# Dense products that read the moving operand's columns alternately from its two halves, with evictions that restore the order

## The chip, the cores and the metric

One core of one Trainium2 chip runs the whole program. The metric is device time of one launch in microseconds, the median of several runs. The core has a matrix engine (TensorE), VectorE, ScalarE and GpSimd, an SBUF of 128 partitions, and a PSUM of 8 banks of 512 fp32 columns in each partition, into which TensorE accumulates.

## The reference

One inference step of one decoder layer, for a prompt of 256 tokens and for 8 sample tokens with the same weights, all in float32:

```
x += 0.5 * SwiGLU_1(RMSNorm(x))                 # 2048 -> 5632 -> 2048
h  = RMSNorm(x);  P = h @ w_in                  # 2048 -> 6400
attention, RWKV-7 time mixing, short convolution, each on its columns of P
x += concat(B_out, A_out, C_out) @ w_out        # 2048 -> 2048
x += 0.5 * SwiGLU_2(RMSNorm(x))
SwiGLU(h) = (silu(h @ w_gate) * (h @ w_up)) @ w_down
```

The outputs are x and the new states. Nearly all arithmetic is in the products with w_gate, w_up, w_down (twice), w_in and w_out; below they are called the dense products.

## The kernel before, in words

Activations lie transposed: a feature is a partition, a token is a column. The 256 prompt tokens and the 8 sample tokens form one row of N = 264 columns. `xr` holds x as 16 tiles of 128 x 264.

Precision is kept by splitting. A weight chunk of up to 4 x 128 rows and 256 columns is loaded into `raw` by SyncE; ScalarE rounds it to `wH` (float32r, L310), VectorE forms the rest `wL = raw - wH` (L365). The activations are split in the same way into `xH`, `xL` (L413, L421), `hH`, `hL` (L473, L477) and `mixH`, `mixL`. A dense product is then three float32r matmuls for each weight tile of 128 x 128: `wH` with the high part (L378), `wH` with the low part (L379), `wL` with the high part (L380). All read 264 moving columns and add into 264 columns of one PSUM bank. `products` issues one chunk: four tiles of rows times two halves of the 256 columns times three, 24 matmuls. The first chunks of w_out go through `ahead_product` (L339) with buffers of their own.

Both functions read the moving operand and write PSUM through views with step -1: the last token first. Since input and output are both reversed, every token still lands in its own column.

Four chunks in ring buffers separate loading, rounding and multiplying; a chunk's consumers wait on the counting semaphores `landed`, `head_made`, `tail_made` and `chunk_used`. All loops are written out by hand for each engine, and an engine works in the order in which its code is written.

Results leave PSUM on VectorE two banks (528 columns) at a time: `gate_scale` (L458) and `hidden` (L466) multiply gate and up by the norm factor `rs`, `project` (L712) does so for w_in's columns into `pj`, `x_add` (L430) adds w_down's and w_out's results to `xr`, and `y_add` (L696) forms the final x in `yf`, which TensorE then transposes (L827, L829) for the output. Gate uses banks 0 and 1, up banks 2 and 3; w_in's pairs alternate between 0 and 2, w_down's and w_out's between 4 and 6. TensorE waits for an eviction only before it begins to overwrite the same banks.

The other matmuls named below are the sums over head dimensions at L1183 (plain fp32, 128 x 264) and the picking of sample values at L1276 (128 weight columns, 4 or 6 moving ones). VectorE's small copies at L979, L1060, L1062, L1381 and L1452 bring transposed columns out of PSUM; L1060 writes into `shT` viewed "p r b -> p b r" (r innermost, 8 elements apart), L1062 into `zs` viewed "p r i b -> p b i r" (r innermost, 24 elements apart), L1452 in runs of four. L1808 reads 264 columns of one bank.

Of the kernel before, what the change touches and what calls it, by code (L numbers as in the profile page):

```python
# [20 lines left out]
ALU = mybir.AluOpType  # L21
# [8 lines left out]
N = T + NB  # L30
# [22 lines left out]
OUT_K0 = (0, 12, 4, 8)  # L53
# [57 lines left out]
def build(nc, t, o):  # L111
# [4 lines left out]
    def at(name, shape, dt, off):  # L116

        return nc.alloc_sbuf_tensor_at(name, shape, dt, offset=base + off)
# [5 lines left out]
    xr = at("xr", [P, KT, N], F32, 49152)  # L124
# [6 lines left out]
    gt = at("gt", [P, 2, N], F32, E0)  # L131
    st = at("st", [P, 2, N], F32, E0 + 2112)
    ut = at("ut", [P, 2, N], F32, E0 + 4224)
# [4 lines left out]
    rs = at("rs", [P, N], F32, K0)  # L138
# [16 lines left out]
    yf = at("yf", [P, 2, 2, N], F32, M0 + 92928 + 6144)  # L155
# [6 lines left out]
    pj = at("pj", [P, MT, N], F32, PB)  # L162
# [81 lines left out]
    def inner_slots(*ks):  # L244
# [18 lines left out]
    ahead = {k: (at(f"wH{k}", [P, CK, CW], F32R, hi), at(f"wL{k}", [P, CK, CW], F32R, lo))  # L263
             for k, hi, lo in ((0, F0, F0 + 8192), (1, F0 + 4096, PB + G), (2, L0 + 4 * HB, L0 + 4 * HB + 4096),
                               (3, L0 + 4 * HB + 8192, L0 + 4 * HB + 12288),
                               (6, PB + 2 * G, PB + 2 * G + 4096), (7, PB + 2 * G + 8192, PB + 2 * G + 12288))}
# [7 lines left out]
    ps = ctx.enter_context(nc.psum_tensor("ps", [P, 8, 512], F32))  # L274
    sems = {}

    def S(name):
        if name not in sems:
            sems[name] = ctx.enter_context(nc.semaphore(name))
        return sems[name]  # L280
# [13 lines left out]
    def number(first, per, i, k):  # L294

        return i * per + (first + k)
# [28 lines left out]
    def pe_ahead(pe, k, qs=range(CK)):  # L325

        pe.wait_ge(S("tail_made"), OUT + k + 1)
        for q in qs:
            for half in range(2):
                ahead_product(k, q, half, 0, mixH, k % 4 == 0 and q == 0)  # L330
                ahead_product(k, q, half, 0, mixL)
                last = ahead_product(k, q, half, 1, mixH, stop=k == 7 and q == CK - 1)
        if CK - 1 in qs:
            last.then_inc(S("chunk_used"), 1)

    def ahead_product(k, q, half, part, mix, start=False, stop=False):

        cols = slice(half * P, half * P + P)
        return nc.tensor.matmul(ps[:, 4 + k // 4 * 2 + half, 0:N][:, ::-1], ahead[k][part][:, q, cols],  # L339
                                mix[:, OUT_K0[k % 4] + q, :][:, ::-1], start=start, stop=stop)  # L340

    def pe_ahead_rwkv(pe):

# [18 lines left out]
    def tail(dve, nk, first, per, i, k):  # L362
# [3 lines left out]
                                wH[:, k % RING, 0:nk, :].bitcast(F32), ALU.subtract  # L366
                                ).then_inc(S("tail_made"), 1)

    def products(pe, vH, vL, k0, nk, bank, start, stop, first, per, i, k):

        pe.wait_ge(S("tail_made"), number(first, per, i, k) + 1)
        for q in range(nk):
            for half in range(2):
                cols = slice(half * P, half * P + P)
                out = ps[:, bank + half, 0:N][:, ::-1]
                high, low = vH[:, k0 + q, :][:, ::-1], vL[:, k0 + q, :][:, ::-1]
                a, b = start and q == 0, stop and q == nk - 1
                nc.tensor.matmul(out, wH[:, k % RING, q, cols], high, start=a, stop=False)  # L378
                nc.tensor.matmul(out, wH[:, k % RING, q, cols], low, start=False, stop=False)  # L379
                last = nc.tensor.matmul(out, wL[:, k % RING, q, cols], high, start=False, stop=b)  # L380
        last.then_inc(S("chunk_used"), 1)

    def two(ap):

        return ap[:].unsqueeze(1).broadcast_to([P, 2, N])
# [6 lines left out]
    def early(q):  # L392

        return isinstance(q, int) and q < 2
# [32 lines left out]
    def x_add(dve, w, q, bank, factor, used):  # L427

        dve.wait_ge(S("chunk_used"), used)
        nc.vector.scalar_tensor_tensor(xr[:, bass.ds(q * 2, 2), :], ps[:, bank:bank + 2, 0:N], factor,  # L430
                                       xr[:, bass.ds(q * 2, 2), :], ALU.mult, ALU.add
                                       ).then_inc(S("x_ready"), 1)

    def norm_sum(pe, w):

# [19 lines left out]

    def gate_scale(dve, u, first, p):
        dve.wait_ge(S("chunk_used"), first + 4 + p * GU_PER)
        nc.vector.tensor_tensor(gt[:], ps[:, 0:2, 0:N], two(rs), ALU.mult).then_inc(S("gate_scaled"), 1)  # L458

    def gate_silu(act, u, p):  # L460
        act.wait_ge(S("gate_scaled"), FT // 2 * u + 1 + p)
# [1 line left out]

    def hidden(dve, u, first, p):
        dve.wait_ge(S("chunk_used"), first + GU_PER + p * GU_PER)
        nc.vector.tensor_tensor(ut[:], ps[:, 2:4, 0:N], two(rs), ALU.mult).then_inc(S("up_scaled"), 1)  # L466
        dve.wait_ge(S("up_scaled"), FT // 2 * u + 1 + p)
        dve.wait_ge(S("silu_made"), FT // 2 * u + 1 + p)
        nc.vector.tensor_tensor(hf[:], st[:], ut[:], ALU.mult).then_inc(S("hidden_made"), 1)
# [171 lines left out]
    def dve_ffn(dve, u, gu, dn):  # L641
        def gate_up(i, first_pair):
            for k in range(RING if first_pair and u == 0 else 0, 4):
                tail(dve, CK, gu, GU_PER, i, k)
            if not first_pair:
                hidden(dve, u, gu, i - 1)
            elif u == 1:
                x_add(dve, 2, KT // 2 - 1, 6, 1.0, GU2)
            tail(dve, CK, gu, GU_PER, i, 4)
            if not first_pair:  # L650
                hidden_tail(dve, u, i - 1)
            elif u == 1:
                x_tails(dve, 2, KT // 2 - 1)
            for k in range(5, GU_PER):
                tail(dve, CK, gu, GU_PER, i, k)
            if first_pair:
                norm_reciprocal(dve, 2 * u)
            gate_scale(dve, u, gu, i)
# [32 lines left out]
    def y_add(dve, q, slot, used):  # L691

        dve.wait_ge(S("chunk_used"), used)
        if not early(q):
            dve.wait_ge(S("y_turned"), q - 1)
        nc.vector.scalar_tensor_tensor(yf[:, slot, :, :], ps[:, 4 + 2 * slot:6 + 2 * slot, 0:N], 0.5,  # L696
                                       xr[:, bass.ds(q * 2, 2), :], ALU.mult, ALU.add
                                       ).then_inc(S("x_ready"), 1)

    def column_pair(q):  # L700

# [2 lines left out]
    def seat(q):  # L704

        return 2 * column_pair(q) + (-6 if 16 <= q < 19 else 6 if q >= 22 else 0)

    def project(dve, q, bank):

        dve.wait_ge(S("chunk_used"), IN + IN_PER + q * IN_PER)  # L710
        c = seat(q)
        nc.vector.tensor_tensor(pj[:, c:c + 2, :], ps[:, bank:bank + 2, 0:N], two(rs), ALU.mult  # L712
                                ).then_inc(S("projected"), 1)

    def dve_in(dve):
        for k in range(4):
            tail(dve, CK, IN, IN_PER, 0, k)
        x_add(dve, 1, KT // 2 - 1, 6, 0.5, IN)
        x_tails(dve, 1, KT // 2 - 1)
        for k in range(4):  # L720
# [55 lines left out]
    def pe_ffn(pe, u, gu, dn):  # L776
        w = 2 * u

        def gate_up(i, first_pair):
            for k in range(GU_PER):  # L780
                if first_pair and k < 4:
                    pe.wait_ge(S("x_tail"), 16 * w + 4 * (k + 1))
                if k == 0 and not first_pair:
                    pe.wait_ge(S("gate_scaled"), FT // 2 * u + i)
                if k == 4 and not first_pair:
                    pe.wait_ge(S("up_scaled"), FT // 2 * u + i)
                products(pe, xH, xL, CK * (k % 4), CK, 0 if k < 4 else 2, k % 4 == 0, k % 4 == 3,
                         gu, GU_PER, i, k)
                if first_pair and u == 0 and k == 0:
                    pe_turn_x(pe, 6)  # L790
                    pe_turn_x(pe, 7)
                if first_pair and k == (5 if u == 0 else 3):
                    norm_sum(pe, w)

        def down(i, jj, first_pair):
            q = i * 2 + jj
            if not (isinstance(i, int) and i == 0):
                pe.wait_ge(S("x_ready"), 8 * (w + 1) - 1 + q)
            for k in range(DN_PER):
                if first_pair:  # L800
                    pe.wait_ge(S("hidden_tail"), FT // 2 * u + (DN_K0[k] + DN_KT[k] + 1) // 2)
                products(pe, hH, hL, DN_K0[k], DN_KT[k], 4 + 2 * jj, k == 0, k == DN_PER - 1,
                         dn + DN_PER * jj, 2 * DN_PER, i, k)
                if u == 1 and not first_pair and k == 5:
                    turn_y(pe, q - 1, 1 - jj)
# [26 lines left out]
    def pe_in(pe):  # L832
        for k in range(4):
            pe.wait_ge(S("x_tail"), 16 + 4 * (k + 1))
            products(pe, xH, xL, CK * k, CK, 0, k == 0, k == 3, IN, IN_PER, 0, k)
# [1651 lines left out]
```

## Time and profile before

| | |
|---|---|
| median of 3 runs | 2109.93 us (2109.79 to 2113.65) |
| span of the profiled execution | 2106.7 us |
| TensorE matmul busy | 2074.8 us, 98% |
| VectorE busy | 1183.1 us, 56% |
| ScalarE busy | 880.0 us, 42% |
| GpSimd busy | 196.9 us, 9% |
| mean granted TensorE clock | 0.994 of 2.4 GHz |
| DMA | 373.43 MB, 177 GB/s mean |

The profile is of one execution; its span, from the first to the last instruction, is what sums are made against. Matmuls are pipelined: an instruction's duration is much longer than the distance to the next one's start, and a busy share of 98% says only that there are few gaps. Weight loads (PEld) run beside the matmul before them.

### The profile page before, as it was taken

What the parts mean: (1) busy time and instruction counts of PE and PEld (TensorE: products, weight loads), DVE (VectorE), ACT (ScalarE), POOL (GpSimd) and SP (SyncE); (2) the same over time, 40 slices, a digit from 0 to 9 for tenths busy, and PEclk for the clock granted to TensorE, in tenths of its full rate; (3) what the DMA queues carried; (4) which work ended last, traced back from release to release, by engine and by line L of the source; (5) the groups of instructions that cost most, each with busy time, mean ns of one, the idle gap of its engine ahead of it and who ended that gap; (6) DMA issues with size and microseconds to landing.
All of it is one profiled execution on the core that took longest, in us unless ns stands there. A gap on an engine that the chain in (4) does not pass through costs nothing.

```text
span 2106.7 us, 44887 instructions
## 1 busy us (share of the span) xinstructions
PE 2074.8 (98%) x18520; PEld 2038.6 (97%) x18520; DVE 1183.1 (56%) x1203; ACT 880.0 (42%) x1004; POOL 196.9 (9%) x160
## 2 busy tenths in 40 slices
PE   8999999999999999999998999999999999999999
PEld 7999999999999999999986899999999999999999
DVE  6555555555444545568996575555555555544443
ACT  5444444444434434434345444444444444433333
POOL 4000000000000000015401871000000000000000
PEclk9999999999999999999998999999999999999999
DMA  5655555665555556668873055555556555556553
GB/s 184 197 182 180 179 180 179 185 182 180 176 179 177 187 172 199 175 201 221 238 237 88 4 165 190 180 180 180 181 179 186 179 179 180 183 166 196 185 176 125
DMA packets 361375, 373.43 MB, mean 177 GB/s; under 512 B 13321, under 2 KB 353837, under 8 KB 361190
## 3 DMA queue, kind: packets, MB, share of 16 engines
q1 hardware_dynamic: 352288, 350.53, 53.5%
q0 software_dynamic: 5424, 15.39, 3.1%
q10 hardware_dynamic: 3582, 6.33, 0.9%
q8 instruction: 63, 1.03, 0.2%
q14 instruction: 18, 0.15, 0.0%
HBM read 366.89 MB, written 5.32 MB: 177 GB/s over the span
## 4 chain that ended last, share of the span: by engine, by line
PE 89%; DVE 5%; DMA 3%; ACT 1%; POOL 1%; issue 1%; ACTq 0%; SPq 0%; POOLq 0%; DVEq 0%
PE ps L378 28%; PE ps L380 28%; PE ps L379 28%; DMA raw<-in_w_in_dram 2%; DVE wL L365 2%; DVE wL L323 1%; POOL acc L888 1%; PE ps L1266 1%; PE ps L1955 0%; DMA vb<-in_cache_swa_v_dram 0%; ACT wH L310 0%; PE ps L1958 0%; DMA xin<-in_x_prompt_dram 0%; PE ps L1966 0%; PE ps L339 0%
## 5 line engine op out<-in xcount | busy, mean ns | idle before, releaser
L365 DVE TENSOR_TENSOR wL<-raw,wH 128x1024 fp32r<-128x1024 f32 (+1 forms) x668 | 824.2, 1240 | 829.3 <-ACT wH L310 828.5
L310 ACT ACTIVATE wH<-raw 128x1024 fp32r<-128x1024 f32 (+1 forms) x668 | 691.2, 1037 | 966.4 <-PE ps L380 888.0
L378 PE MATMUL ps<-xH,wH 128*128 128x264 f32 x3616 | 1030.2, 285 | 6.2 <-DVE wL L365 5.8
L380 PE MATMUL ps<-xH,wL 128*128 128x264 f32 x3616 | 1027.3, 284 | 0.0
L379 PE MATMUL ps<-xL,wH 128*128 128x264 f32 x3616 | 1027.2, 284 | 0.0
L378 PEld LDWEIGHTS ps<-xH,wH 128*128 128x128 f32 x3616 | 681.3, 188 | 11.3 <-issue 9.7
L380 PEld LDWEIGHTS ps<-xH,wL 128*128 128x128 f32 x3616 | 681.1, 188 | 0.0
L379 PEld LDWEIGHTS ps<-xL,wH 128*128 128x128 f32 x3616 | 680.5, 188 | 0.2
L378 PE MATMUL ps<-hH,wH 128*128 128x264 f32 x1408 | 402.4, 286 | 0.0
L380 PE MATMUL ps<-hH,wL 128*128 128x264 f32 x1408 | 401.4, 285 | 0.0
L379 PE MATMUL ps<-hL,wH 128*128 128x264 f32 x1408 | 401.3, 285 | 0.0
L378 PEld LDWEIGHTS ps<-hH,wH 128*128 128x128 f32 x1408 | 265.0, 188 | 0.2
L379 PEld LDWEIGHTS ps<-hL,wH 128*128 128x128 f32 x1408 | 265.1, 188 | 0.0
L380 PEld LDWEIGHTS ps<-hH,wL 128*128 128x128 f32 x1408 | 264.6, 188 | 0.0
L462 ACT ACTIVATE st<-gt 128x528 f32<-128x528 f32 x44 | 28.5, 647 | 83.6 <-DVE gt L458 83.6
L888 POOL TENSOR_TENSOR acc<-acc,sq 128x528 f32<-128x528 f32 x21 | 34.9, 1663 | 278.0 <-ACT sq L406 277.0
L378 PE MATMUL ps<-mixH,wH 128*128 128x264 f32 x192 | 54.5, 284 | 0.0
L379 PE MATMUL ps<-mixL,wH 128*128 128x264 f32 x192 | 54.5, 284 | 0.0
L380 PE MATMUL ps<-mixH,wL 128*128 128x264 f32 x192 | 54.5, 284 | 0.0
L890 POOL COPY acc<-sq 128x528 f32<-128x528 f32 x3 | 2.7, 894 | 552.5 <-ACT sq L406 549.7
L421 DVE SCALAR_TENSOR_TENSOR xL<-xr,vcol,xH 128x264 fp32r<-128x264 f32 (+1 forms) x48 | 29.9, 664 | 15.6 <-ACT xH L413 15.4
L380 PEld LDWEIGHTS ps<-mixH,wL 128*128 128x128 f32 x192 | 36.1, 188 | 0.0
(377 smaller groups left out, 1140.3 us busy)
## 6 DMA issues: line engine op xcount, KB each, us to landing
raw<-in_ffn_w_gate_dram SPq DMA_DIRECT2D x176, 512.0 KB, 3.5
raw<-in_ffn_w_up_dram SPq DMA_DIRECT2D x176, 512.0 KB, 3.5
raw<-in_ffn_w_down_dram SPq DMA_DIRECT2D x128, 512.0 KB, 3.3
raw<-in_w_in_dram SPq DMA_DIRECT2D x100, 512.0 KB, 4.9
raw<-in_ffn_w_down_dram SPq DMA_DIRECT2D x64, 384.0 KB, 2.8
raw<-in_w_out_dram SPq DMA_DIRECT2D x32, 512.0 KB, 4.4
kb<-in_cache_swa_k_dram POOLq DMA_DIRECT2D x24, 256.0 KB, 6.6
vb<-in_cache_swa_v_dram ACTq DMA_DIRECT2D x24, 256.0 KB, 6.4
```

Source lines behind the costliest of these rows:

```text
L310: nc.scalar.activation(wH[:, k % RING, 0:nk, :], raw[:, k % RING, 0:nk, :], ACT.Copy).then_inc(S("head_made"), 1)
L323: nc.vector.tensor_tensor(low[:], raw[:, k % RING], high[:].bitcast(F32), ALU.subtract).then_inc(S("tail_made"), 1)
L365: nc.vector.tensor_tensor(wL[:, k % RING, 0:nk, :], raw[:, k % RING, 0:nk, :], wH[:, k % RING, 0:nk, :].bitcast(F32), ALU.subtract).then_i ...
L378: nc.tensor.matmul(out, wH[:, k % RING, q, cols], high, start=a, stop=False)
L379: nc.tensor.matmul(out, wH[:, k % RING, q, cols], low, start=False, stop=False)
L380: last = nc.tensor.matmul(out, wL[:, k % RING, q, cols], high, start=False, stop=b)
L421: nc.vector.scalar_tensor_tensor(xL[:, bass.ds(q * 2 + e, 1), :], xr[:, bass.ds(q * 2 + e, 1), :], vcol[:, 0, bass.ds(q * 2 + (16 * w + e) ...
L462: nc.scalar.activation(st[:], gt[:], ACT.Silu).then_inc(S("silu_made"), 1)
L888: nc.gpsimd.tensor_tensor(acc[:], acc[:], sq[:, slot, :, :], ALU.add).then_inc(S("squares_added"), 1)
L890: nc.gpsimd.tensor_copy(acc[:], sq[:, 0, :, :]).then_inc(S("squares_added"), 1)
L1266: last = nc.tensor.matmul(ps[rows, 4, :], pS[:, g, b, :], vb[:, b % 3, g, :], start=g == 0, stop=g == 2)
```

## The change

Two views replace the reversed ones. The moving operand is read as token 0, token 132, token 1, token 133, and so on; PSUM is written in ascending order, so column 2c + w of a bank holds token 132w + c. Each eviction reads its banks with step 2 and writes natural order. `x_add` and `y_add`, which had one instruction for two banks, now have one for each bank.

```diff
@@ ahead_product
-        return nc.tensor.matmul(ps[:, 4 + k // 4 * 2 + half, 0:N][:, ::-1], ahead[k][part][:, q, cols],
-                                mix[:, OUT_K0[k % 4] + q, :][:, ::-1], start=start, stop=stop)
+        return nc.tensor.matmul(ps[:, 4 + k // 4 * 2 + half, 0:N].rearrange("p (c way) -> p c way", way=2), ahead[k][part][:, q, cols],
+                                two_ways(mix[:, OUT_K0[k % 4] + q, :]), start=start, stop=stop)
@@
+    def two_ways(ap):
+
+        return ap.rearrange("p (way c) -> p c way", way=2)
+
+    def by_token(bank):
+
+        return ps[:, bank:bank + 2, 0:N].rearrange("p e (c way) -> p e way c", way=2)
+
+    def by_way(ap):
+
+        return ap.rearrange("p e (way c) -> p e way c", way=2)
+
@@ products
-                out = ps[:, bank + half, 0:N][:, ::-1]
-                high, low = vH[:, k0 + q, :][:, ::-1], vL[:, k0 + q, :][:, ::-1]
+                out = ps[:, bank + half, 0:N].rearrange("p (c way) -> p c way", way=2)
+                high, low = two_ways(vH[:, k0 + q, :]), two_ways(vL[:, k0 + q, :])
@@ x_add
-        nc.vector.scalar_tensor_tensor(xr[:, bass.ds(q * 2, 2), :], ps[:, bank:bank + 2, 0:N], factor,
-                                       xr[:, bass.ds(q * 2, 2), :], ALU.mult, ALU.add
-                                       ).then_inc(S("x_ready"), 1)
+        for e in range(2):
+            tile = by_way(xr[:, bass.ds(q * 2 + e, 1), :])[:, 0]
+            last = nc.vector.scalar_tensor_tensor(tile, by_token(bank)[:, e], factor, tile, ALU.mult, ALU.add)
+        last.then_inc(S("x_ready"), 1)
@@ gate_scale
-        nc.vector.tensor_tensor(gt[:], ps[:, 0:2, 0:N], two(rs), ALU.mult).then_inc(S("gate_scaled"), 1)
+        nc.vector.tensor_tensor(by_way(gt[:]), by_token(0), by_way(two(rs)), ALU.mult).then_inc(S("gate_scaled"), 1)
@@ hidden
-        nc.vector.tensor_tensor(ut[:], ps[:, 2:4, 0:N], two(rs), ALU.mult).then_inc(S("up_scaled"), 1)
+        nc.vector.tensor_tensor(by_way(ut[:]), by_token(2), by_way(two(rs)), ALU.mult).then_inc(S("up_scaled"), 1)
@@ y_add
-        nc.vector.scalar_tensor_tensor(yf[:, slot, :, :], ps[:, 4 + 2 * slot:6 + 2 * slot, 0:N], 0.5,
-                                       xr[:, bass.ds(q * 2, 2), :], ALU.mult, ALU.add
-                                       ).then_inc(S("x_ready"), 1)
+        for e in range(2):
+            last = nc.vector.scalar_tensor_tensor(by_way(yf[:, slot])[:, e], by_token(4 + 2 * slot)[:, e], 0.5,
+                                                  by_way(xr[:, bass.ds(q * 2 + e, 1), :])[:, 0], ALU.mult, ALU.add)
+        last.then_inc(S("x_ready"), 1)
@@ project
-        nc.vector.tensor_tensor(pj[:, c:c + 2, :], ps[:, bank:bank + 2, 0:N], two(rs), ALU.mult
+        nc.vector.tensor_tensor(by_way(pj[:, c:c + 2, :]), by_token(bank), by_way(two(rs)), ALU.mult
                                 ).then_inc(S("projected"), 1)
```

## Rows read from the trace of the kernel before

**Rows 1.** The page: busy time by engine, and TensorE's clock in 40 slices.
```profile
PE 2074.8 (98%) x18520; PEld 2038.6 (97%) x18520; DVE 1183.1 (56%) x1203; ACT 880.0 (42%) x1004; POOL 196.9 (9%) x160
PEclk9999999999999999999998999999999999999999
```

**Rows 2.** Waits of all engines: who waited for whom, total us, times, longest.
```profile
DVE wL L365 <- ACT wH L310: 828.5, 575, 6.1
...
PE ps L378 <- DVE wL L365: 5.8, 5, 2.5
```

**Rows 3.** Groups of TensorE instructions: shapes, count, busy us, mean ns, idle before.
```profile
L378 PE MATMUL ps<-xH,wH 128*128 128x264 f32 x3616 | 1030.2, 285 | 6.2 <-DVE wL L365 5.8
...
L378 PE MATMUL ps<-hH,wH 128*128 128x264 f32 x1408 | 402.4, 286 | 0.0
...
L378 PE MATMUL ps<-mixH,wH 128*128 128x264 f32 x192 | 54.5, 284 | 0.0
...
L339 PE MATMUL ps<-mixH,wH 128*128 128x264 f32 x64 | 16.2, 292 | 2.1 <-DVE wL L323 2.0
```

**Rows 4.** Stretches: length, PE, PEld, DVE, ACT, POOL busy (instructions), clock, DMA, GB/s.
```profile
100.00:535.00 435.00, 435.00 (x3602) 435.00 (x3601) 231.09 (x224) 179.14 (x187) 0.00 (x0) 1.00 0.59 181
560.00:900.00 340.00, 340.00 (x2786) 339.61 (x2785) 173.62 (x160) 139.87 (x151) 16.40 (x14) 1.00 0.58 179
...
1340.00:1830.00 490.00, 490.00 (x4056) 489.97 (x4056) 263.00 (x255) 202.69 (x213) 0.00 (x0) 1.00 0.59 181
```

**Rows 5.** Timeline of TensorE around 1000 us: start, duration, instruction.
```profile
999.75 0.28 PE L378 MATMUL ps<-xH,wH 128*128 128x264 f32 x1
999.87 0.28 PE L379 MATMUL ps<-xL,wH 128*128 128x264 f32 x1
999.99 0.28 PE L380 MATMUL ps<-xH,wL 128*128 128x264 f32 x1
```

**Rows 6.** The plain fp32 product L1183: its group, and eight records in the timeline.
```profile
L1183 PE MATMUL ps<-rq,cb 128*128 128x264 f32 x16 | 3.9, 386 | 0.0
...
886.86 1.94 PE L1183 MATMUL ps<-rq,cb 128*128 128x264 f32 x8
```

**Rows 7.** Timeline of L1276, four moving columns under 128 weight columns.
```profile
1141.44 0.96 PEld L1276 LDWEIGHTS ps<-cb,vm 64*128 64x128 f32 x8 [0.34 <-issue]
1141.44 1.05 PE L1276 MATMUL ps<-cb,vm 64*128 64x4 f32 x8
```

**Rows 8.** Groups of VectorE: the five evictions, and one of 264 columns.
```profile
L458 DVE TENSOR_TENSOR gt<-ps,rs 128x528 f32<-128x528 f32 x44 | 30.8, 700 | 0.1
L466 DVE TENSOR_TENSOR ut<-ps,rs 128x528 f32<-128x528 f32 x44 | 30.8, 700 | 0.0
...
L712 DVE TENSOR_TENSOR pj<-ps,rs 128x528 f32<-128x528 f32 x25 | 17.5, 700 | 11.4 <-PE ps L380 11.3
...
L430 DVE SCALAR_TENSOR_TENSOR xr<-ps,xr 128x528 f32 x12 | 8.4, 700 | 0.0
...
L696 DVE SCALAR_TENSOR_TENSOR yf<-ps,xr 128x528 f32<-128x528 f32 x8 | 5.6, 702 | 6.9 <-PE ps L380 6.9
...
L1808 DVE SCALAR_TENSOR_TENSOR kk<-ps,vcol,pj 128x264 f32<-128x264 f32 x6 | 2.5, 482 | 0.0
```

**Rows 9.** Groups of VectorE: small copies out of PSUM.
```profile
L1060 DVE COPY shT<-ps 128x160 f32<-128x160 f32 x1 | 0.4, 444 | 0.0
L1452 DVE COPY pS<-ps 128x96 f32<-128x96 f32 x2 | 0.4, 248 | 0.0
...
L1062 DVE COPY zs<-ps 128x96 f32<-128x96 f32 x1 | 0.4, 369 | 0.0
...
L1381 DVE COPY qkr<-ps 96x128 f32<-96x128 f32 x1 | 0.3, 277 | 0.0
...
L979 DVE COPY vcol<-ps 128x68 f32<-128x68 f32 x1 | 0.2, 219 | 0.0
```

**Rows 10.** Timeline of the end: the last eviction.
```profile
2101.39 0.71 DVE L696 SCALAR_TENSOR_TENSOR yf<-ps,xr 128x528 f32<-128x528 f32 x1 [6.95 <-PE ps L380]
```

## The prediction, made before the changed kernel was built or timed

> **What bounds the kernel now.** I read the page first: TensorE is busy 98% of the 2106.7 us span, at full clock in almost every slice [rows 1]. Busy does not mean at its peak, so I next asked who waits for whom [rows 2]: VectorE waits 828.5 us for ScalarE's rounded weights before L365, while the dense products wait for VectorE's split weights five times, 5.8 us in all. So nothing feeds TensorE late; the kernel is as long as its instruction stream.
>
> The stream is then a count times a spacing. The groups of instructions [rows 3] show L378 three times (first operand xH, hH and mixH); L379 and L380 are issued as often, so the count is 3 x (3616 + 1408 + 192) = 15648, and the products of L339 add 3 x 64 = 192: 15840. The 284 to 292 ns beside them are not the price, since the instructions overlap. The price is the distance between two starts: in the timeline 0.12 us [rows 5], and over long stretches at clock 1.00, 435.00 us for 3602 instructions (0.1208 us each), 340.00 for 2786 (0.1220) and 490.00 for 4056 (0.1208) [rows 4]. I take 0.1215. 15840 x 0.1215 = 1925 us, 91% of the span. What the change does to this one number decides everything: 1 ns of spacing is 15.8 us.
>
> **What the 121.5 ns are made of.** Two neighbours show what the pieces can do. The plain fp32 products at L1183 read the same 264 columns, forwards. There are 8 matmuls in the code and 16 records, so each record holds half a matmul; eight records take 1.94 us, and with the last one 0.386 long their starts are (1.94 - 0.386)/7 = 0.222 us apart [rows 6]. I read a record as two passes over 264 columns, as fp32 needs more than one: 111 ns a pass, or 264 columns at the 2.4 GHz level (110 ns). The other neighbour is L1276, whose moving operand has 4 columns and whose weights are 128 columns of fp32: its eight weight loads take 0.96 us with the last 0.19 long, so (0.96 - 0.19)/7 = 0.110 us each [rows 7]. Weight loading alone thus keeps the dense stream above 110 ns, streaming alone above 111, and it runs at 121.5. About 10 ns are left that neither explains; the reversed read, the reversed write, or two reads of SBUF at a time can be their cause.
>
> **Part 1, the moving read (L339, L376).** Before, neighbours in the stream are neighbours in SBUF, read backwards. After, the stream jumps by 132 columns (528 bytes) and back at every element; no two elements that follow each other are near each other. No TensorE instruction of the trace reads that way at length, so the price is bounded from both sides.
>
> From VectorE I have what a large step can cost. A 68-column and a 128-column copy out of PSUM take 219 and 277 ns, 0.97 ns an element. The copy at L1060 moves 160 elements and writes each 32 bytes from the last; by that slope it would take 277 + 32 x 0.97 = 308 ns, and it took 444: 0.85 ns more for each element. The copy at L1062 writes 96 elements 96 bytes apart and took 369 ns where L1452, as large and written in runs of four, took 248: 1.26 ns more [rows 9]. So steps of 32 and 96 bytes roughly double an element's time on that engine. These are writes and another engine, so they show that SBUF minds the step, not TensorE's price. Its upper bound from them is 0.97 + 0.85 to 0.97 + 1.26 = 1.82 to 2.23 ns a column, 480 to 589 ns a matmul. The lower bound is below nothing: the 10 unexplained ns may go, down to 112 ns.
>
> Between the ends I take a halved rate: 264 columns at the 1.2 GHz level, 220 ns, and with the 2 ns that L1183's records have over their columns 222 ns. The same factor of two is what the step cost on VectorE, and it is what would come out if TensorE could fetch one distant element in the time in which it now fetches two neighbours. At 222.5 ns the weight load (110) and everything else hide below the stream. Sum: 15840 x (0.2225 - 0.1215) = +1600 us.
>
> The Trainium skill has a rule for this: "SBUF — State Buffer", section "Door 1: The DMA port swizzle", says that SBUF is read in lines of 16 bytes, that at least two hits on a line are needed to hide its latency, and that steps beyond 4 fp32 are no longer free. By that rule the new order has no second hit and loses; the rows of VectorE agree in kind. The skill gives no factor for TensorE.
>
> **Part 2, the PSUM write.** Both the old and the new output are contiguous; the new one ascends. Gain or loss within the unexplained 10 ns; taken at 0, since the read sets the pace in the forecast.
>
> **Part 3, the evictions.** They now read PSUM every second element (8 bytes apart) and write SBUF in two runs of 132. The three full-width forms take 700 ns for 528 elements, x44, x44 and x25; x_add (16 in the code, 12 in the row) and y_add (8) take 700 ns [rows 8]; the last are split in two of 264 elements, for which L1808 (482 ns, 264 elements out of PSUM) is the nearest row: 0.96 instead of 0.70 us, +0.26. If an 8-byte step costs nothing, VectorE gets 24 x 0.26 = 6 us more. If it costs 1.26 ns an element as at L1062, +0.67 us on all 137 evictions and 6 besides: 98 us. I take it near nothing, because it is the shortest step of all. Either way it lies beside TensorE: the gate, up and projection banks are double-buffered, an eviction is awaited only some four chunks (of 24 matmuls, 2.9 us) later, and VectorE waits over 800 us at L365. It is on the path only where a stage must have the last eviction: the start of w_in's products, the last projection, the start of the second FFN, and the last y_add, after which TensorE turns the result [rows 10]. Four places, at +0.26 us (at most +0.93): 1 us, at most 4. If TensorE gave back its 10 ns, a chunk would still last 2.7 us against 1.27 us of VectorE for its weights, so the cover stays.
>
> No DMA, semaphore or queue moves, so no wait is added; in the forecast the 5.8 us of waits for VectorE vanish.
>
> **Sum.** 2106.7 + 1600 + 1 - 6 = 3702 us span. The median before (2109.9) is 3.2 us over the profiled span: 3705 us.
>
> **The rivals.**
> - The step is hidden by lines kept open or banks read in parallel, at a small fee. The two halves lie 528 bytes apart, and a short stretch fetched for one column would still hold the next columns of its half, only alternately. Anything from 125 to 210 ns, 2165 to 3510 us. Against it: VectorE's rows show no such mercy. For it: those streams never come back to a stretch, and this one does, two columns later.
> - Worse than half, at VectorE's strided 1.82 ns a column, 480 ns: 2110 + 15840 x 0.3585 = 7790 us.
> - The change does nothing to the stream, because the 10 ns belong to the handing over of the weights (they appear when load and stream are nearly equal, 110 and 111 ns) and TensorE does not mind steps: 2110 + 1 to 4 = 2111 to 2114 us.
> - It is faster. Mechanism: the 10 ns are a conflict between the moving read and the weight load, each a run over SBUF, and alternating between two distant places spreads it; or the backward order itself costs them, since L1183 forwards at 111 ns a pass does not show them. It wins from the point where TensorE can take two distant columns in the time of two neighbours. Full gain 15840 x (0.1215 - 0.112) = 150 us, 1960 us; half of it, 2035 us. For it: the spacing is 0.1208 us in one stretch and 0.1220 in another at the same clock [rows 4], so something beside the array touches it. The Trainium skill, "TensorE: Matmul & The Clock Gate", section "Back-to-back issue gap", gives N/2.4 + 2.5 ns for a lone stream, 112.5 ns here; the trace disagrees by 9 ns, and if the rule held after the change the time would be the full gain's.
>
> **How the numbers follow.** Halved rate, 3500 to 3900 us (209 to 235 ns; the top keeps the extra 10 ns over 222): 0.50. Small fee: 0.10. Worse than half: 0.07. Nothing: 0.12. Faster: 0.21, of which 0.04 below 1990. The likeliest is 3705 us, its own range 3500 to 3900. The range over all cases, 1990 to 3900, leaves out 0.07 above and 0.04 below. Faster by over 0.2% 0.21, within 0.2% 0.12, slower 0.67; 0.2% is about what a measurement of this kernel can tell from no change.
>
> **What would show it.** Right: the start-to-start distance at L378 to L380 near 0.222 us at clock 1.00, VectorE's share falling to about 32%, the DMA rate to about 100 GB/s, L1183 unchanged at 0.222. Evictions stay at 0.70 us, the halves at 0.48; 1.2 us and more would show a price for the 8-byte step. Wrong: a spacing of 112 to 125 ns. A lower granted clock would be another cause than the one I price.

## The result, and the profile after

The change makes the kernel faster: 1988.24 us median (1984.76 to 1996.85) against 2109.96 us, a ratio of 0.9425 with a 95% interval of 0.9403 to 0.9447. The forecast was 3705 us, and the range began at 1990. All times below are of runs at the same high granted clock (0.987 or more over the whole run); one run of `write_backward`, 2298.87 us at 0.824, is left out.

The page of the kernel after, busy time and clock (columns as in [rows 1]):

```profile
PE 1941.8 (98%) x18520; PEld 1904.8 (96%) x18520; DVE 1184.1 (60%) x1227; ACT 881.8 (44%) x1004; POOL 196.4 (10%) x160
PEclk9999999999999999999998999999999999999999
```

The span is 1984.7 us. TensorE is as full as before and at the same clock; VectorE has 24 instructions and 1 us more. So it is the stream of dense products itself that got shorter. Stretches of the kernel after (columns as in [rows 4]) and its timeline around 1000 us (as [rows 5]):

```profile
100.00:500.00 400.00, 400.00 (x3558) 400.00 (x3557) 228.14 (x221) 178.55 (x186) 0.00 (x0) 1.00 0.64 194
530.00:730.00 200.00, 200.00 (x1780) 200.00 (x1780) 106.33 (x110) 89.24 (x102) 11.81 (x7) 1.00 0.60 194
1340.00:1730.00 390.00, 390.00 (x3469) 390.00 (x3468) 223.08 (x217) 174.24 (x182) 0.00 (x0) 1.00 0.64 194
```
```profile
999.88 0.28 PE L390 MATMUL ps<-xH,wH 128*128 128x264 f32 x1
999.99 0.28 PE L391 MATMUL ps<-xL,wH 128*128 128x264 f32 x1
1000.10 0.28 PE L392 MATMUL ps<-xH,wL 128*128 128x264 f32 x1
```

400.00/3558 = 0.1124 us from start to start, 0.1124 in the other two, where [rows 4] gave 0.1208 and 0.1220. Of these 112.4 ns, 110.0 are what 264 columns take at the 2.4 GHz level. The unevenness is gone too: the three stretches agree to 0.1 ns.

15840 products x (0.1215 - 0.1124) would be 144 us; the span fell by 122. Where most of the other 22 went shows when the dense stages are laid side by side. Before, then after, each from its first to its last dense product: gate and up 1, down 1, w_in, w_out (without its first chunks), gate and up 2, down 2:

```profile
16.00:535.00 519.00, 515.33 (x4237) 513.66 (x4236) 285.83 (x277) 220.70 (x238) 20.59 (x21) 1.00 0.59 180
536.00:793.00 257.00, 257.00 (x2108) 257.00 (x2107) 125.14 (x120) 104.30 (x118) 11.83 (x7) 1.00 0.56 178
794.00:1120.00 326.00, 316.50 (x2559) 303.94 (x2557) 241.25 (x266) 131.33 (x148) 61.72 (x65) 0.99 0.71 208
1258.00:1327.00 69.00, 69.00 (x573) 69.00 (x572) 40.65 (x44) 34.00 (x43) 8.73 (x7) 1.00 0.62 194
1328.00:1838.00 510.00, 510.00 (x4219) 509.87 (x4218) 273.70 (x265) 212.38 (x224) 1.82 (x1) 1.00 0.59 181
1839.00:2101.00 262.00, 262.00 (x2154) 261.69 (x2153) 111.08 (x103) 96.60 (x108) 0.00 (x0) 1.00 0.53 172
```
```profile
17.00:502.00 485.00, 479.98 (x4239) 478.37 (x4238) 285.64 (x277) 221.93 (x237) 20.52 (x21) 1.00 0.63 192
503.00:739.00 236.00, 236.00 (x2100) 236.00 (x2100) 124.75 (x127) 103.95 (x118) 11.81 (x7) 1.00 0.60 193
740.00:1060.00 320.00, 302.90 (x2575) 289.94 (x2574) 241.21 (x268) 132.37 (x150) 61.43 (x65) 0.98 0.72 212
1196.00:1260.00 64.00, 64.00 (x570) 64.00 (x570) 40.90 (x50) 33.86 (x43) 8.69 (x7) 1.00 0.65 207
1261.00:1736.00 475.00, 475.00 (x4221) 474.87 (x4220) 273.38 (x266) 214.33 (x224) 1.82 (x1) 1.00 0.64 195
1737.00:1979.00 242.00, 242.00 (x2154) 241.69 (x2154) 111.51 (x110) 96.48 (x108) 0.00 (x0) 1.00 0.58 186
```

The lengths fell by 34, 21, 6, 5, 35 and 20 us, 121 in all. Each stage gave about what its count promises except w_in's (gate and up, for instance: 4224 products x (0.1208 - 0.1124) = 35 us). Its 2400 dense products at about 9 ns less promise some 22 us, and 6 came. There attention's scores and the sample caches share the stage. Its middle, after:

```profile
895.00:1006.00 111.00, 99.04 (x841) 96.72 (x839) 104.62 (x95) 43.89 (x56) 42.53 (x43) 0.97 0.83 238
```

For 111 us it is VectorE that is full (104.62 us busy) and TensorE that waits (12 us idle), where before that held for 45 us only:

```profile
965.00:1010.00 45.00, 38.92 (x316) 37.99 (x315) 42.68 (x30) 22.05 (x33) 17.87 (x15) 1.00 0.77 214
```

Over the whole stage TensorE's idle time, length less busy, grew from 9.5 to 17.1 us. TensorE, with less to do there, waits for VectorE for longer. Its clock gives some back too. In two stretches after, the granted clock was 0.83, between its two levels, where no stretch between 794 and 1090 us of the kernel before was below 1.00:

```profile
905.00:915.00 10.00, 9.70 (x71) 9.73 (x72) 7.59 (x7) 9.65 (x20) 3.72 (x4) 0.83 0.86 268
945.00:955.00 10.00, 8.42 (x61) 8.46 (x62) 10.00 (x10) 3.93 (x5) 0.52 (x1) 0.83 0.70 220
```

In the 10 us before each of them TensorE was busy for 6.31 and 8.32 us. As an estimate, a mean of 0.83 is a third of the stretch at the 1.2 GHz level, which costs 1.7 us each, 3.4 us together. With the 7.6 us more of idle time that is 11 of the 16 us; for the rest no row gives a cause. A wait shorter than a matmul's own duration does not show as idle. The wait list of the whole kernel after names the split of the weights (what TensorE waited for: us in total, times, longest; the line of before is in [rows 2]), and the chain of waits of this stretch, by line, adds the transfers of w_in to it:

```profile
PE ps L390 <- DVE wL L365: 12.3, 10, 2.9
```
```profile
by line: DVE wL L365 40.9%; DMA raw<-in_w_in_dram 33.3%; ACT sc L1319 4.9%; ACT wH L310 4.7%; DVE ss L1433 4.5%; DVE pj L1097 2.2%; DVE am L1420 2.1%; DVE sc L1422 2.1%; DVE sc L1419 2.0%; DVE sc L1428 1.7%; DVE pj L726 1.7%; issue 1.2%; AC
```

The transfers wait for a ring slot that VectorE's split has to free, and the split for the transfer: the two in turn hold three quarters of the chain, and TensorE's products next to none of it. The same loop stands in the kernel before, in its shorter stretch from 965 to 1010 us (39.8% and 35.1% of the chain). That it is what kept most of the 16 us is read from these rows; no kernel was run for it.

The evictions after, the lines that answer [rows 8]:

```profile
L471 DVE TENSOR_TENSOR gt<-ps,rs 128x528 f32<-128x528 f32 x44 | 30.9, 701 | 0.1
L479 DVE TENSOR_TENSOR ut<-ps,rs 128x528 f32<-128x528 f32 x44 | 30.8, 701 | 0.0
...
L726 DVE TENSOR_TENSOR pj<-ps,rs 128x528 f32<-128x528 f32 x25 | 17.5, 700 | 10.8 <-PE ps L392 10.7
...
L444 DVE SCALAR_TENSOR_TENSOR xr<-ps,xr 128x264 f32 x24 | 9.2, 424 | 0.0
...
L710 DVE SCALAR_TENSOR_TENSOR yf<-ps,xr 128x264 f32<-128x264 f32 x16 | 6.1, 425 | 6.3 <-PE ps L392 6.3
...
L444 DVE SCALAR_TENSOR_TENSOR xr<-ps,xr 128x264 f32<-128x264 f32 x8 | 3.1, 423 | 0.0
```

The step of 8 bytes in PSUM costs VectorE nothing (701 against 700 ns), and a half takes 424 ns. The halves overlap a little, so that the split adds less than 2 x 424 - 700 ns each time: the busy time of these groups is 9.2 + 6.1 + 3.1 = 18.4 us, against 8.4 + 5.6 in [rows 8] and 2.8 us for the other four of x_add, together 16.8. That is 1.6 us more.

### The profile page after: what moved, and what is told of

It is laid out like the page before. It is cut to its first block, busy times and chain, and to the rows that moved or that the text cites. A ratio compares the mean times of both kernels' runs of the same rounds, so it can differ in the third digit from the quotient of the medians.

```text
span 1984.7 us, 44915 instructions
## 1 busy us (share of the span) xinstructions
PE 1941.8 (98%) x18520; PEld 1904.8 (96%) x18520; DVE 1184.1 (60%) x1227; ACT 881.8 (44%) x1004; POOL 196.4 (10%) x160
## 4 chain that ended last, share of the span: by engine, by line
PE 88%; DVE 5%; DMA 4%; ACT 1%; POOL 1%; issue 1%; ACTq 0%; SPq 0%; DVEq 0%; POOLq 0%
PE ps L390 27%; PE ps L392 27%; PE ps L391 27%; DMA raw<-in_w_in_dram 3%; DVE wL L365 3%; DVE wL L323 1%; POOL acc L902 1%; PE ps L1280 1%; PE ps L1969 0%; ACT wH L310 0%; PE ps L1972 0%; DMA xin<-in_x_prompt_dram 0%; DMA vb<-in_cache_swa_v_dram 0%; ACTq L1340 0%; PE ps L1980 0%
## 5 line engine op out<-in xcount | busy, mean ns | idle before, releaser
L390 PE MATMUL ps<-xH,wH 128*128 128x264 f32 x3616 | 1004.0, 278 | 12.3 <-DVE wL L365 12.3
L392 PE MATMUL ps<-xH,wL 128*128 128x264 f32 x3616 | 1000.0, 277 | 0.0
L391 PE MATMUL ps<-xL,wH 128*128 128x264 f32 x3616 | 1000.0, 277 | 0.0
L390 PE MATMUL ps<-hH,wH 128*128 128x264 f32 x1408 | 389.2, 276 | 0.0
L391 PE MATMUL ps<-hL,wH 128*128 128x264 f32 x1408 | 388.6, 276 | 0.0
L392 PE MATMUL ps<-hH,wL 128*128 128x264 f32 x1408 | 388.6, 276 | 0.0
L390 PEld LDWEIGHTS ps<-mixH,wH 128*128 128x128 f32 x192 | 36.3, 189 | 0.0
```

## The experiments

### Twenty streams, side by side

The theories at the start were three. "Direction": walking backwards cost the extra 9 ns. "Spread": moving read and weight load hinder each other unless the reads are spread. "Sixteen bytes": steps cost. The first kernel adds streams of 24 dense products after the last work of the kernel before, each on its own source line:

```diff
+        for w, x, y, s, e in sets(128):
+            nc.tensor.matmul(y[:, 0:264], w, x[:, 0:264], start=s, stop=e)
+        for w, x, y, s, e in sets(128):
+            nc.tensor.matmul(y[:, 0:264][:, ::-1], w, x[:, 0:264][:, ::-1], start=s, stop=e)
+        for w, x, y, s, e in sets(128):
+            nc.tensor.matmul(y[:, 0:264].rearrange("p (c way) -> p c way", way=2), w, x[:, 0:264].rearrange("p (way c) -> p c way", way=2), start=s, stop=e)
...
```

> The kernel before, with 20 streams of 24 dense products each added after its last instruction of work, in the same pattern of weights and moving tiles (wH with hH, wH with hL, wL with hH), written to a PSUM bank that nobody reads. Each stream differs in one thing: the order of the moving read, the order of the PSUM write, the width of the row (264 or 256) or of the weights (128 or 64 columns). Measured is the start-to-start distance of each. Theory 'direction': walking backwards costs the 8 to 10 ns; forward read and forward write gives 112 ns, backward both gives 120, and one of the two mixed streams names the culprit. Theory 'spread': two runs over SBUF, the moving read and the weight load, get in each other's way wherever neighbours are read in turn; then forward gives 120 or more too, as do steps of 2, and only orders whose neighbours are distant (two, four and eight ways, steps of 33) give 112; with 64 weight columns, so half the weight load, the backward stream falls towards 112. Theory 'sixteen bytes': if steps cost TensorE anything, the step of 33 and the two ways stand above the others; under both other theories they cost nothing. If the weight load is the new floor, two ways with 64 weight columns still gives 112 only if streaming 264 columns needs it as well.

Measured is (start of the 24th - start of the 1st)/23. Two of the pairs of rows, first and last of two ways and of eight ways:

```profile
2115.42 0.27 PE L2423 MATMUL ps<-hH,wH 128*128 128x264 f32 x1
...
2118.00 0.28 PE L2423 MATMUL ps<-hH,wL 128*128 128x264 f32 x1
...
2152.34 0.40 PE L2437 MATMUL ps<-hH,wH 128*128 128x264 f32 x1
...
2157.62 0.41 PE L2437 MATMUL ps<-hH,wL 128*128 128x264 f32 x1
```

2.58/23 = 112.2 ns and 5.28/23 = 229.6 ns. All of them in this way, each from one execution; the orders that were run twice agree to 1 ns once a first gap is left out:

| moving read | PSUM write | ns between starts |
|---|---|---|
| forward | forward | 121.3 (the first time 124.8, with a first gap of 210) |
| backward | backward | 121.3 (121.7 in the repeat) |
| backward | forward | 121.3 |
| forward | backward | 121.3 |
| two ways (0, 132, 1, 133, ...) | ascending | 112.2 |
| four ways (steps of 66) | ascending | 142 in its part at clock 1.00 |
| eight ways (steps of 33) | ascending | 229.6 (230.0 in another stream) |
| steps of 2 / 4 / 6 / 12 columns | ascending | 238 / 240 / 234 / 322 |
| 256 columns: forward / backward / two ways | same | 119 / 117 / 112 |
| 64 weight columns: forward / backward / two ways | same | 121.3 / 121.3 / 112.6 |

"Direction" falls: all four mixtures of direction agree. "Spread" falls too, though forwards at over 120 ns fitted it: four and eight ways have distant neighbours as well and take 142 and 230 ns, and with half the weight load nothing changes, so the extra 9 ns are no quarrel with the weight load. Two ways stay at 112.6 with 64 weight columns, so it is the 264 columns and not the weights that set that floor. Steps do cost, as "sixteen bytes" had it, about double, and more at 12 columns; but already 2 columns cost it, and two alternating places cost nothing and win.

The rows hold one more thing. In the middle of the stream with steps of 12 columns the granted clock fell to the 1.2 GHz level, after TensorE had been busy without a gap, and the starts kept their distance:

```profile
2147.00:2148.00 1.00, 1.00 (x4) 1.00 (x4) 0.00 (x0) 0.00 (x0) 0.00 (x0) 0.50 0.00 0
```
```profile
2147.13 0.52 PE L2433 MATMUL ps<-hH,wL 128*128 128x264 f32 x1
2147.45 0.51 PE L2433 MATMUL ps<-hH,wH 128*128 128x264 f32 x1
2147.77 0.52 PE L2433 MATMUL ps<-hL,wH 128*128 128x264 f32 x1
```

They are 0.32 us apart, as at clock 1.00. So the pace of that order is not set by the clock that is granted to TensorE. Where the clock is low and the order cheaper, columns over clock decide: the first six starts of the four ways, still at 0.50, are 0.22 us apart (264 columns at 1.2 GHz take 0.220), the later ones 0.142.

### The directions in the whole kernel

```diff
-                out = ps[:, bank + half, 0:N][:, ::-1]
-                high, low = vH[:, k0 + q, :][:, ::-1], vL[:, k0 + q, :][:, ::-1]
+                out = ps[:, bank + half, 0:N]
+                high, low = vH[:, k0 + q, :], vL[:, k0 + q, :]
...
```

(`ahead_product` likewise)

> The kernel before with neither view reversed: moving operand read forwards, PSUM written forwards, evictions as before. Theory 'direction': 112.5 ns spacing and 1985 to 1990 us, all of the gain without touching an eviction. Theory 'spread': spacing 120 ns or more, 2100 to 2250 us.

2123.94 us, ratio 1.0059 (1.0042 to 1.0076): a little slower than backwards. The two mixed kernels reverse one side alone, and the evictions read PSUM backwards (`ps[:, bank:bank + 2, 0:N][:, :, ::-1]`).

> The moving operand read backwards as before, PSUM written forwards, each eviction reading its banks backwards. If the backward PSUM write is what costs, 112.5 ns and about 1985 us; if the read side sets the pace, 121 ns and about 2107 us as before.

2109.78 us, 0.9993 (0.9984 to 1.0003): the backward write of the kernel before cost nothing.

> The moving operand read forwards, PSUM written backwards, each eviction reading its banks backwards. If the backward write costs, 121 ns and about 2107 us. If only the read matters, the time equals that of the forward kernel, whatever that is.

2123.33 us, the median of three runs, 1.0064 (1.0044 to 1.0084), the same as forward. So of the two directions only the read's matters, and in the whole kernel forwards is the dearer way. One stretch of `forward`, then the same of `read_backward`:

```profile
1340.00:1830.00 490.00, 490.00 (x3999) 489.87 (x3998) 259.57 (x252) 201.37 (x213) 1.82 (x1) 1.00 0.58 178
```
```profile
1340.00:1830.00 490.00, 490.00 (x4054) 489.87 (x4053) 262.75 (x254) 202.73 (x213) 0.00 (x0) 1.00 0.58 181
```

0.1225 against 0.1209 us. Alone, without other engines and transfers, both took 0.1213. These 1.6 ns are 14 us over about 8400 gate and up products, the whole of the 13 to 14 us. What makes them is open.

### What the reader minds: distance, runs, ways

A second kernel of streams asks what makes two ways good.

```diff
+        nc.tensor.matmul(y[:, 0:256].rearrange("p (b c way) -> p b c way", way=2, c=4), w, x[:, 0:256].rearrange("p (b way c) -> p b c way", way=2, c=4), start=s, stop=e)
+        nc.tensor.matmul(y[:, 0:264].rearrange("p (c way r) -> p c way r", way=2, r=2), w, x[:, 0:264].rearrange("p (way c r) -> p c way r", way=2, r=2), start=s, stop=e)
...
```

> The kernel before with 25 other streams of 24 products each behind its work, measured as before by the distance of their starts; all write PSUM in ascending order. The first streams gave 121 ns for any contiguous order, 112 for two ways and 230 to 320 for steps. Theory 'neighbours held': the reader fetches a short stretch and holds two of them; alternating between two far stretches lets one be fetched while the other serves. Then two ways at any distance that lies outside one stretch gives 112 (8, 16, 32, 64 columns apart), 2 or 4 apart stands higher, runs of 2 or 4 columns from each half give 112 to 121, runs of 12 about 121, and six ways is as bad as eight, 230. Theory 'distance': what matters is which bank of SBUF the next element is in; then the result jumps about with the distance (64 against 66, 128 against 132) and not with the number of ways. Rows of 512: if the extra 9 ns are per column, 512 forward takes 216 + 17 = 233 ns and two ways 216; if they are per instruction, 225. Rows of 128: the weight load sets 112 for both orders. Plain fp32: 222 a record forwards; if each column is read once for two passes, the step of 33 still gives 222, if it is read for each pass, 440 or more.

First and last rows of two ways at 4 columns' distance, of runs of 2, and of two ways over 512 columns:

```profile
2117.21 0.27 PE L2425 MATMUL ps<-hH,wH 128*128 128x256 f32 x1
...
2119.77 0.28 PE L2425 MATMUL ps<-hH,wL 128*128 128x256 f32 x1
```
```profile
2104.07 0.33 PE L2417 MATMUL ps<-hH,wH 128*128 128x264 f32 x1
...
2107.99 0.35 PE L2417 MATMUL ps<-hH,wL 128*128 128x264 f32 x1
```
```profile
2165.83 0.38 PE L2457 MATMUL ps<-hH,wH 128*128 128x512 f32 x1
...
2170.80 0.38 PE L2457 MATMUL ps<-hH,wL 128*128 128x512 f32 x1
```

2.56/23 = 111.3, 3.92/23 = 170.4 and 4.97/23 = 216.1 ns. All:

| read | ns between starts |
|---|---|
| two ways, 2 columns (8 bytes) apart | 118.7 |
| two ways, 4 / 8 / 16 / 32 / 64 apart (256 columns) | 111.3 / 111.7 / 111.7 / 111.7 / 111.7 |
| two ways 132 apart / the same, both walked backwards | 112.2 / 112.6 |
| runs of 2 / 4 / 12 columns from each half in turn | 170.4 / 132.2 / 126.5 |
| four ways, 66 / 64 apart | 142.2 / 140.9 |
| six ways, 44 apart | 150.9 |
| forward, from column 1 / from column 2 (256 columns) | 120.4 / 120.9 |
| 128 columns: forward / two ways | 109.1 / 111.7 |
| 512 columns: forward / two ways | 233.9 / 216.1 |
| plain fp32, a record: forward / steps of 33 | 222.6 / 460.7 |

"Distance" falls: 132 and 4 apart give the same; from 16 bytes on, distance has no meaning. The extra is per column (9 ns at 264, 18 at 512), and at 128 columns nothing of it is seen (109.1 forwards), beside a weight load of 110 ns. "Neighbours held" got the distances from 8 columns on right and put the limit too far out: it had 4 columns apart stand higher, and they took 111.3. The short runs it had wrong: it said 112 to 121 for runs of 2 and 4, and they took 170 and 132; six ways should have been as bad as eight and took 151 against 230. So what is shown is narrower than that theory: two places read strictly in turn, at least 16 bytes apart, run within 3 ns of what the columns at 2.4 GHz or the weight load (110 ns) ask for; no other order tried with 256 columns or more does. How the reader fetches so that it comes out this way is not settled. If a record of plain fp32 is two passes, as the prediction read it, then its row says that each pass reads again (460.7 is twice 230), and that fp32 forwards, 111.3 a pass, does not pay the 9 ns that float32r pays. Why it does not stays open.

### The forecast's own price, met in another order

```diff
-        return ap.rearrange("p (way c) -> p c way", way=2)
+        return ap.rearrange("p (way c) -> p c way", way=8)
...
```

> The changed kernel with 4 in place of 2 in every view: the moving operand is read at token 0, 66, 132, 198, 1, and so on, and the evictions restore that order. Its stream took 143 ns alone. Theory 'neighbours held', with room for two stretches: 143 ns or somewhat more, 2107 + 15840 x 0.0215 = 2450 us. If only the fact of alternating between distant places counts, 112 ns and 1985 us.

2431.01 us, ratio 1.1513 (1.1489 to 1.1536). It is the 143 ns that hold, and not the mere alternating: its stretch from 100 to 500 us has 2806 instructions, 0.1426 us each.

> The same with 8: steps of 33 columns. Its stream took 230 ns alone, near the 222 ns that the prediction took for two ways. Then 2107 + 15840 x 0.1085 = 3825 us, VectorE's waits for ScalarE grow, and the evictions stay hidden even with a PSUM step of 32 bytes.

3868.11 us, ratio 1.8318 (1.8281 to 1.8355). A stretch of the eight ways, and VectorE's line for the eviction of gate:

```profile
100.00:500.00 400.00, 400.00 (x1708) 358.37 (x1707) 110.07 (x108) 85.72 (x89) 0.00 (x0) 1.00 0.30 93
```
```profile
L471 DVE TENSOR_TENSOR gt<-ps,rs 128x528 f32<-128x528 f32 x44 | 30.8, 700 | 0.1
```

0.2342 us between starts at full clock, DMA at 93 GB/s, and an eviction that reads PSUM in steps of 32 bytes still takes 700 ns. VectorE is busy for 31% of the span, as the forecast said (32%). This is nearly the profile that the forecast described, only with 234 ns in place of 222, for a read that comes back to a stretch after eight columns and not after two.

### The parts of the change, and the distance under load

```diff
-                out = ps[:, bank + half, 0:N]
-                high, low = vH[:, k0 + q, :], vL[:, k0 + q, :]
+                out = ps[:, bank + half, 0:N].rearrange("p (c way) -> p c way", way=2)
+                high, low = vH[:, k0 + q, :].rearrange("p (way c) -> p c way", way=2), vL[:, k0 + q, :].rearrange("p (way c) -> p c way", way=2)
...
```

(shown against the forward kernel, whose evictions are those of before; `ahead_product` likewise; `four_apart` has "p (b way c) -> p b c way" with c=4 in its place)

> Only the matmul part of the change: two-way read, ascending write, with the evictions of the kernel before, so the tokens end in the wrong columns. If the evictions cost nothing on the path, it takes the time of the change, 1988 us within 0.3%. If they cost what the bound of the prediction allowed, up to 4 us less.

1987.36 us, ratio 0.9414 (0.9398 to 0.9430).

> The dense products read, within each group of 8 tokens, 0, 4, 1, 5, 2, 6, 3, 7: two ways only 16 bytes apart, all over the row; PSUM written ascending, evictions of the kernel before, so the tokens end in the wrong columns. Alone such a stream took 112 ns. Theory 'neighbours held' (two short stretches fetched alternately, the distance without meaning once they are different stretches): 112.5 ns under load as well and 1985 to 1990 us. Theory 'distance' (the halves must lie far apart so as not to meet other traffic of SBUF): 116 ns or more under load, 2030 us and more.

1987.93 us, ratio 0.9414 (0.9399 to 0.9430), and the same stretch as the change:

```profile
100.00:500.00 400.00, 400.00 (x3558) 400.00 (x3558) 228.43 (x222) 178.20 (x185) 0.00 (x0) 1.00 0.64 194
```

> The change itself on the chip of the two kernels above, as their measure: 1988 us, 112.4 ns between starts in the FFN stages.

1987.32 us, ratio 0.9410 (0.9395 to 0.9426). All three agree: the gain is the read order alone, the evictions cost nothing that can be measured, and 16 bytes are as good as 528 under load too. The opposite combination, forward products with the evictions of the change:

> The kernel after with the matmul views of the forward kernel (read and written in order) but the evictions of the change, so the tokens end in the wrong columns. Against the forward kernel (ratio 1.006 to the kernel before) it prices the evictions alone. If they cost nothing on the path, the same 2124 us within 0.2%; if the step of 8 bytes or the split adds cost on the path, up to 4 us more. The eviction's duration should be 0.70 us.

2124.83 us, ratio 1.0058 (1.0042 to 1.0075), as `forward` with 1.0059.

## Why the prediction was wrong, point by point

- **What bounds the kernel: right.** The stream's spacing decided everything. 15840 products and 1 ns of spacing for 15.8 us held but for the 22 us of 144 that did not come, 16 of them in w_in's stage.
- **What the spacing is made of: right in size.** 10 ns were left over 111; 9 of them went. The causes that were offered for them are refuted: the weight load, as conflict or as handing over, by the streams with 64 weight columns (121.3 ns still) and by the 18 ns that 512 columns pay beside one load; the backward read by `forward`, 0.6% slower; the backward write by `read_backward`. What does cause them is open. That L1183 reads forwards at 111 ns a pass was no evidence on float32r, which takes 121 forwards.
- **Part 1, the step that failed.** "Between the ends I take a halved rate": +101 ns for each dense product, where the change brought -9.1 (0.1215 to 0.1124 us). The price was taken from VectorE copies that write each element far from the last and never return; about the same factor is found on TensorE, but in other orders (230 ns at eight ways, 238 at steps of 2 columns). Here each second element is again a neighbour. That difference was written down, under the first rival, and given 0.10. Two ends so far apart, with no row of TensorE between them, did not bear 0.50 on one value between them. The rule of the Trainium skill ("SBUF — State Buffer", section "Door 1: The DMA port swizzle") pulled the same way, and the measurements contradict it for this read: alternating between two 16-byte lines at every element is the fastest order of all, while a step of 2 columns, with two hits on each line, costs as much (238 ns) as a step of 4 (240).
- **Part 2, the write: right**, at 0 (`read_backward` 0.9993).
- **Part 3, the evictions: right.** The step of 8 bytes was taken near nothing and is nothing; the split came to 1.6 us of VectorE where 6 were expected, because a half takes 0.424 us and not 0.48, and two in a row overlap. Their cover held. The excess at L1060 and L1062 fits their stepped write to SBUF, since both read PSUM in order; no run separates it.
- **The cover of the faster case was read too coarsely.** "A chunk would still last 2.7 us against 1.27 us of VectorE" holds in the FFN; in w_in's stage VectorE carries attention as well and the weights' ring waits for it, and there 16 of 22 us were given back. Of the 28 us by which even the rival's full gain, 1960 us, was missed, 16 are these and 6 are the floor of 0.1124 us in place of 0.112. With both in the sum the full gain would have stood at 1982 us, still outside the range: that began at 1990 because only 0.04 of the 0.21 for faster lay below it.
- **The rival that came true** had 0.21. "It wins from the point where TensorE can take two distant columns in the time of two neighbours" is what happened; its spacing of 0.112 us was met with 0.1124 us in the kernel. But both mechanisms that it offered, the conflict with the weight load and the backward order, are refuted above. It had the size right without the reason. The Trainium skill, "TensorE: Matmul & The Clock Gate", section "Back-to-back issue gap", gives N/2.4 + 2.5 ns, which is 112.5 ns here. These runs agree for the read in two ways (112.2 to 112.4 ns), and not for the contiguous one (121.3).

## What to carry to other kernels

Count the matmuls, take the distance between starts from a long stretch, and compare it with columns over clock: where float32r products of 256 columns or more stand some 10% above that, try reading the moving operand from two places in turn, at least 16 bytes apart, with PSUM written in order and the order restored in the eviction. Do not generalise from "steps are dear": the price hangs on the whole pattern (112, 142, 230 ns for two, four, eight ways), and a stream of 24 products appended to a kernel measures it. Only float32r rows of 128 to 512 columns were tried; at 128 there was nothing to gain. A gain on the bounding engine is paid out stage by stage; where another engine is already near full in one stage, expect that stage to keep it.

## What the runs showed of the hardware that was not expected

- TensorE took 121.3 ns for a contiguous float32r row of 264 columns and 233.9 for one of 512, and 112.2 and 216.1 ns when two places were read in turn. The columns alone are 110.0 and 213.3 ns at the 2.4 GHz level.
- Steps of 2, 4, 6 and 33 columns cost 230 to 240 ns for 264 columns, steps of 12 columns 322, and that was the same when the granted clock fell to 0.50.
- A record of plain fp32 took 222.6 ns contiguous and 460.7 with steps of 33 columns, twice what a float32r product takes in that order (230).
- VectorE read PSUM in steps of 8 and of 32 bytes as fast as contiguously (701 and 700 ns for 528 elements, 700 before).
